# Loading x and the first projection's weights in six pairs of transfers, with the rope angles and the sum over x moved later

## The reference, cut to what matters

```python
h = rms_norm(x, attn_pre_g[0])
a = h @ w_a                                   # 1024 -> 384 + 256 + 64
cq, ckv, kr = jnp.split(a, [384, 640], axis=-1)
q  = (rms_norm(cq, g_q) @ w_uq) ...           # rope on part of it
kv = (rms_norm(ckv, g_kv) @ w_ukv) ...
ang = positions[..., None] * inv              # rope tables
cos, sin = jnp.cos(ang), jnp.sin(ang)
```

## Time and profile before

| | us |
|---|---|
| median of 3 runs | 982.19 |
| lowest and highest run | 981.73, 982.43 |
| span of the profiled execution | 980.3 |
| TensorE busy in the span | 958.4 (98%) |
| DVE busy | 720.6 (74%) |
| ACT busy | 542.4 (55%) |

### The profile page before, as it was taken

One profiled execution on the slowest core, in us unless ns is written; L12 is line 12 of the kernel. 1 busy time (PEld: TensorE's weight loads), 2 busy tenths in 40 slices (PEclk: granted clock), 3 DMA queues, 4 the chain that ended last, 5 costly groups with the idle time before them and its releaser, 6 DMA issues.

```text
span 980.3 us, 18888 instructions
## 1 busy us (share of the span) xinstructions
PE 958.4 (98%) x7971; PEld 923.9 (94%) x7971; DVE 720.6 (74%) x1340; ACT 542.4 (55%) x837; POOL 25.4 (3%) x54
## 2 busy tenths in 40 slices
PE   8999999999999999999999999999999999999997
PEld 8889999999998988899999997998999999999996
DVE  7965897777658777698879788555654879888653
ACT  7554664454447366565444545456755567666542
POOL 0300000000000000000000000000220000000000
PEclk9999999999999999999999999999999999999999
DMA  8536376766744734368767882653343545555621
GB/s 298 190 116 238 128 266 255 255 251 225 295 172 168 266 129 140 116 212 304 265 251 267 331 315 76 245 185 116 111 149 132 199 157 207 181 203 184 216 87 43
DMA packets 27588, 194.72 MB, mean 199 GB/s; under 512 B 3056, under 2 KB 3184, under 8 KB 4592
## 3 DMA queue, kind: packets, MB, share of 16 engines
q1 hardware_dynamic: 27504, 193.51, 54.7%
HBM read 192.45 MB, written 1.05 MB: 197 GB/s over the span
## 4 chain that ended last, share of the span: by engine, by line
PE 89%; ACT 4%; DVE 4%; issue 2%; DMA 1%; POOL 0%; SPq 0%; DVEq 0%; ACTq 0%
PE bank L508 25%; PE bank L509 24%; PE bank L514 23%; PE bank L639 2%; PE bank L665 2%; PE bank L569 2%; PE bank L563 2%; ACT s_whi L906 2%; PE bank L564 2%; PE bank L528 2%; PE bank L535 1%; PE bank L529 1%; PE bank L649 1%; DVE s_wlo L1382 1%; DMA s_xT<-in_xT 1%
## 5 line engine op out<-in xcount | busy, mean ns | idle before, releaser
L1382 DVE TENSOR_TENSOR s_wlo<-s_raw,s_whi 128x512 fp32r<-128x512 f32 (+1 forms) x364 | 372.3, 1065 | 138.1 <-ACT s_whi L906 137.9
L906 ACT ACTIVATE s_whi<-s_raw 128x1024 fp32r<-128x1024 f32 (+2 forms) x233 | 304.8, 1335 | 215.6 <-PE bank L514 205.9
L508 PE MATMUL bank<-s_hh,s_whi 128*128 128x256 f32 x1400 | 393.6, 281 | 1.1 <-DVE s_wlo L1382 0.7
L509 PE MATMUL bank<-s_hl,s_whi 128*128 128x256 f32 x1400 | 387.6, 277 | 0.0
L514 PE MATMUL bank<-s_hh,s_wlo 128*128 128x256 f32 x1383 | 382.8, 277 | 0.0
L508 PEld LDWEIGHTS bank<-s_hh,s_whi 128*128 128x128 f32 x1400 | 263.3, 188 | 6.9 <-issue 5.9
L509 PEld LDWEIGHTS bank<-s_hl,s_whi 128*128 128x128 f32 x1400 | 263.2, 188 | 0.1
L514 PEld LDWEIGHTS bank<-s_hh,s_wlo 128*128 128x128 f32 x1383 | 259.8, 188 | 0.0
L508 PE MATMUL bank<-s_ph,s_whi 128*128 128x256 f32 x528 | 146.4, 277 | 0.0
L509 PE MATMUL bank<-s_pl,s_whi 128*128 128x256 f32 x528 | 145.8, 276 | 0.0
L514 PE MATMUL bank<-s_ph,s_wlo 128*128 128x256 f32 x516 | 142.5, 276 | 0.0
(11 more groups left out here) (238 smaller groups left out, 1285.3 us busy)
## 6 DMA issues: line engine op xcount, KB each, us to landing
s_raw<-in_gu SPq DMA_DIRECT2D x44, 1024.0 KB, 4.9
s_raw<-in_dn SPq DMA_DIRECT2D x33, 1024.0 KB, 4.9
s_raw<-in_wada SPq DMA_DIRECT2D x24, 1024.0 KB, 5.7
s_raw<-in_up SPq DMA_DIRECT2D x22, 1024.0 KB, 4.9
s_raw<-in_wo SPq DMA_DIRECT2D x8, 1024.0 KB, 4.9
s_raw<-in_win_g SPq DMA_DIRECT2D x8, 1024.0 KB, 4.9
s_raw<-in_mla SPq DMA_DIRECT2D x4, 1024.0 KB, 5.4
s_raw<-in_wkv_v SPq DMA_DIRECT2D x4, 1024.0 KB, 4.9
```

The costliest lines, as they stand in the source:

```text
L508: e.matmul(out, hi, xh[:, k, :], start=first, stop=False, skip_group_check=True)
L509: e.matmul(out, hi, xl[:, k, :], start=False, stop=False, skip_group_check=True)
L906: e.activation(whi[w % SPLIT][:, at], raw[p % RAW][:, at], ACT.Copy).then_inc(S.hi.tick((w, c0)), 1)
L1382: e.tensor_tensor(wlo[s][:, at], raw[p % RAW][:, at], whi[s][:, at].bitcast(F32), ALU.subtract).then_inc(S.lo.tick((i, j), (i, "all")), 1)
```

## The change

x and the weights of `wa` pieces 0 and 1 come in six pairs of transfers, one pair for each of the chunks 0, 1, 2, 3 and one for 4 and 5 and for 6 and 7; ACT and DVE wait for the pair that they need. The positions move behind x and come in a transfer of their own behind the sixth pair. `WARM` is 12 instead of 16. On ACT the squares of x come between the high parts of piece 2, and sine and cosine behind them. On DVE `x_low` follows each low part of pieces 0 and 1; the angle steps come with chunks 6 and 7 and between the low parts of piece 2, and the sum of squares between and behind those. TensorE's `sums("x0", 7)` moves from behind `lead` to the middle of output tile 5. The layout in on-chip memory behind `xT` stays where it was.

```diff
@@ -39,8 +39,10 @@
...
 NFIRST = 9
-WARM = 16
-FRONT = 16 + T
+WARM = 12
+FRONT = 16
+BLOCKS = ((0, 1), (1, 2), (2, 3), (3, 4), (4, 6), (6, 8))
+BLOCK_OF = {k: b for b, (k0, k1) in enumerate(BLOCKS) for k in range(k0, k1)}
 MLA = ([("wuk", i) for i in range(4)] + [("wuq", i) for i in range(12)] +
@@ -327,9 +329,9 @@
...
         wlo = [sb(f"wlo{i}", [P, PIECE * P], F32R) for i in range(SPLIT)]
-        x_front = sb("xT", [P, FRONT + 8 * T])
-        xT = x_front[:, FRONT:].rearrange("p (a b) -> p a b", a=8)
-        shift(960 + 1024 - 4 * FRONT)
+        x_front = sb("xT", [P, FRONT + 9 * T])
+        xT = x_front[:, FRONT:FRONT + 8 * T].rearrange("p (a b) -> p a b", a=8)
+        shift(960 - 4 * FRONT)
         hh = sb("hh", [P, 8, T], F32R)
@@ -352,7 +354,7 @@
...
         banks = [ctx.enter_context(nc.psum_tensor(f"bank{i}", [P, 512], F32)) for i in range(8)]
-        cosb, sinb, posi = adacc[:, 0:T], adacc[:, T:2 * T], x_front[:, FRONT - T:FRONT].bitcast(I32)
+        cosb, sinb, posi = adacc[:, 0:T], adacc[:, T:2 * T], x_front[:, FRONT + 8 * T:FRONT + 9 * T].bitcast(I32)
         sqb = [yb[:, 2 * i:2 * i + 2, :] for i in range(4)]
@@ -403,10 +405,11 @@
...
         S.cols_in = signal("cols_in", 16)
-        S.x_in = [signal(f"x_in{i}", 16) for i in range(2)]
+        S.x_in = [signal(f"x_in{i}", 16) for i in range(len(BLOCKS))]
+        S.pos_in = signal("pos_in", 16)
         S.relb_in, S.relm_in, S.c_in = signal("relb_in", 16), signal("relm_in", 16), signal("c_in", 16)
         S.raw_in = [signal(f"raw_in{i}", 16) for i in range(RAW)]
-        S.first_in = signal("first_in", 16)
+        S.first_in = [signal(f"first_in{i}", 16) for i in range(len(BLOCKS))]
         S.out_stored = signal("out_stored", 16)
@@ -448,8 +451,13 @@
...
             q = Once(e, counted)
-            first = FRONT + 2 * T
-            e.dma_start(x_front[:, 0:first], a["xT"][:, 0:first]).then_inc(S.x_in[0].tick("x"), 16)
+            for b, (k0, k1) in enumerate(BLOCKS):
+                x_at = slice(FRONT + k0 * T if k0 else 0, FRONT + k1 * T)
+                piece, w_at = k0 // 4, slice(k0 % 4 * 512, k0 % 4 * 512 + (k1 - k0) * 512)
+                src = a["wa"][:, piece * PIECE * P * P:(piece + 1) * PIECE * P * P].rearrange("a (p n) -> (a p) n", p=P)
+                e.dma_start(x_front[:, x_at], a["xT"][:, x_at]).then_inc(S.x_in[b].tick("x"), 16)
+                e.dma_start(raw[piece][:, w_at], src[:, w_at]).then_inc(S.first_in[b].tick(b), 16)
+            e.dma_start(x_front[:, FRONT + 8 * T:], a["xT"][:, FRONT + 8 * T:]).then_inc(S.pos_in.tick("pos"), 16)
             last = {name: WEIGHTS[of[-1]] for name, of in OF.items()}
@@ -460,11 +468,7 @@
...
                 dst = raw[i % RAW]
-                if i == 0:
-                    e.dma_start(dst[:, 0:1024], src[:, 0:1024]).then_inc(S.first_in.tick(0), 16)
-                    e.dma_start(x_front[:, first:], a["xT"][:, first:]).then_inc(S.x_in[1].tick("x"), 16)
-                    e.dma_start(dst[:, 1024:2048], src[:, 1024:2048]).then_inc(S.raw_in[0].tick(0), 16)
-                else:
+                if i >= 2:
                     e.dma_start(dst[:, 0:k * P], src).then_inc(S.raw_in[i % RAW].tick(i), 16)
@@ -536,7 +540,7 @@
...
 
-            def tiles(name, n, m, nk, xh, xl, made, b, by, last=0, seven=None):
+            def tiles(name, n, m, nk, xh, xl, made, b, by, last=0, seven=None, between=None):
 
@@ -551,6 +555,8 @@
...
                                 event if k == nk - 1 else None, name in HALVED and j == 0 and k == 1 and n % HALVED[name] == 0)
+                        if between is not None and j == 0 and k == 3:
+                            between()
 
@@ -681,9 +687,8 @@
...
             lead("wa", 4, 8, hh, hl, "h0", (0, 1), S.dve_out)
-            sums("x0", 7, acc=1)
             tiles("wa", 4, 1, 8, hh, hl, "h0", 2, S.dve_out)
-            tiles("wa", 5, 2, 8, hh, hl, "h0", 3, S.dve_out)
+            tiles("wa", 5, 2, 8, hh, hl, "h0", 3, S.dve_out, between=lambda: sums("x0", 7, acc=1))
             tiles("wuk", 0, 2, 2, cqh, cql, "cq", 4, S.dve_out)
@@ -896,8 +901,9 @@
...
                 p = WEIGHTS[w]
-                if w == 0 and i < 2:
-                    q.wait_ge(S.first_in, 0)
+                if w < 2:
+                    b = BLOCK_OF[4 * w + c0 // 4]
+                    q.wait_ge(S.first_in[b], b)
                 else:
@@ -1018,37 +1024,32 @@
...
             def x_high(k):
-                q.wait_ge(S.x_in[0 if k < 2 else 1], "x")
+                q.wait_ge(S.x_in[BLOCK_OF[k]], "x")
                 e.activation(hh[:, k, :], xT[:, k, :], ACT.Copy, scale=col("pre0", k)).then_inc(S.xhi.tick(("h0", k)), 1)
...
 
-            x_high(0)
-            x_high(1)
-            hi_part(2)
-            hi_part(2)
-            for k in range(2, 6):
+            for k in range(4):
                 x_high(k)
-            hi_part(2)
-            hi_part(2)
-            x_high(6)
-            x_high(7)
+                hi_part(2)
+            for k in (4, 6):
+                x_high(k)
+                hi_part(2)
+                x_high(k + 1)
+            hi_part(3)
+            x0_square(0)
+            x0_square(1)
+            hi_part(3)
+            x0_square(2)
+            x0_square(3)
             q.wait_ge(S.rot, "angle")
...
             e.activation(cosb, tmp[0][:, :], ACT.Sin, scale=-1.0, bias=epsc[:, 1:2]).then_inc(S.trig.tick("cos"), 1)
-            x0_square(0)
-            hi_part(2)
-            hi_part(2)
-            x0_square(1)
-            x0_square(2)
-            hi_part(3)
-            x0_square(3)
-            hi_part(3)
             log_tables()
@@ -1520,7 +1521,7 @@
...
                 if i == 0:
-                    q.wait_ge(S.x_in[0], "x")
+                    q.wait_ge(S.pos_in, "pos")
                     m = e.tensor_copy(r_[:, :], posi)
@@ -1537,26 +1538,25 @@
...
             def x_low(k):
-                q.wait_ge(S.x_in[0 if k < 2 else 1], "x")
+                q.wait_ge(S.x_in[BLOCK_OF[k]], "x")
                 low_scaled(xT[:, k, :], col("pre0", k), hh[:, k, :], hl[:, k, :], "h0", k)
 
-            angle(0)
-            angle(1)
-            x_low(0)
+            for k in range(8):
+                lo_part(2)
+                x_low(k)
+                if k >= 6:
+                    angle(k - 6)
+            lo_part(3)
             angle(2)
-            x_low(1)
-            lo_part(1)
             angle(3)
-            lo_part(1)
-            for k in range(2, 6):
-                x_low(k)
-                angle(k + 2)
-            lo_all(1)
-            x_low(6)
-            x_low(7)
-            lo_all(2)
-            for i in (1, 2, 3):
-                square_sum("x0", i, sqv[i])
+            lo_part(3)
+            for i in range(4, 8):
+                angle(i)
+            lo_part(3)
+            square_sum("x0", 1, sqv[1])
+            lo_part(3)
+            square_sum("x0", 2, sqv[2])
+            square_sum("x0", 3, sqv[3])
             fold("x0")
@@ -2098,7 +2098,7 @@
...
     pos = np.broadcast_to(f["positions"][0].astype(np.int32).view(np.float32)[None, :], (P, T))
-    o["xT"] = np.concatenate([o["cols"][:, :NFIRST], np.zeros((P, FRONT - T - NFIRST), np.float32), pos, x], axis=1)
+    o["xT"] = np.concatenate([o["cols"][:, :NFIRST], np.zeros((P, FRONT - NFIRST), np.float32), x, pos], axis=1)
     wa = f["mla_w_a"][0]
```

## The result

| | before | changed |
|---|---|---|
| median of 6 runs each, us | 982.58 | 986.97 |
| lowest and highest run | 981.73, 983.17 | 983.93, 990.59 |
| span of the profiled execution | 980.3 | 981.7 |
| time of the changed kernel's profiled execution | | 983.93 |
| TensorE busy, DVE busy, ACT busy in the span | 958.4, 720.6, 542.4 | 956.2, 721.5, 542.9 |

The ratio is 1.0043 [1.0024, 1.0063]: slower by 0.4%, where 983.1 and "no difference" had been forecast, and outside the range. Two things stand out. The runs of the changed kernel spread over 6.7 us, those of before over 1.4. And the profiled execution is the fastest of the six, only 1.4 us of span above that of before. So these two profiles show 1.4 of the 4.4 us, and the rest must be looked for in other executions.

The account below looks back on a forecast made before the run. TensorE, busy 98% of the span, bounds the kernel; only its waits can change. The 3.7 us won in `lead` are lost at `wuk`; scores come 0.95 later, so span 980.3 gives 981.3, plus 1.9 is 983.1; range 980.8 to 985.2.

Parts of the forecast that it names:

- TensorE's lead: TensorE in `lead`: it ends at 17.6 instead of 21.3, taken alone a gain of 3.7 us.
- the two new waits: TensorE stands 1.7 us before the sums of x in tile 5 and 2.8 us before `wuk`.
- The chain from the fold: DVE and ACT to `wuk`: fold ends 23.3, R 25.0, `low_rank(0)` 1.4 later, `wuk` at 30.5 instead of 29.91.
- read as 16 us: Skill's 2.0 us fixed per DMA: eight more transfers, one behind the other, would cost some 16 us; not adopted.
- the transfers "at nothing": Start of the queue: bytes give the landings, thirteen issues cost nothing, the queue stays full, piece 2 still at 14.9.
- the last weights of pair 4: Transfers in `lead`: pair 4 ends at 2312 KB, interpolated to land at 10.2 us.
- The row it had leaned on: Price of 1 KB rows: 158.5 KB transfer landed at 15.3 while the queue moved 467 GB/s, so nothing extra.
- rival A: From pair 4's landing: small transfers are paid for, 1.6 us for piece 2, so 984.8; chance 0.15.
- the first product: TensorE's start on x: the first product at about 5.6 instead of 7.8 us.
- The scores: TensorE's first scores, after DVE's stretch behind `wuk`: 44.55 instead of 43.60, later by 0.95 us.
- rival B: Wait before `wuk`: TensorE's clock falls from 2.4 to 1.2 GHz, up to 1.5 us more, so 984.6; chance 0.04.
- Behind the scores: Rest of the kernel: nothing found that could give the delay back, since each stage waits for TensorE.

Follow-up runs that it names:

- r6: Changed kernel's new order of work with the five old transfers of the kernel before: 986.54 us, ratio 1.0040.
- r9: Changed kernel with unread matmuls in all three waits (7 before the sums of x, 11 before `wuk`, 9 before the scores): 984.46 us, ratio 1.0015.
- r2: Changed kernel with 16 unread matmuls at the start instead of 12: 987.15 us, ratio 1.0044.
- r4: Changed kernel with 7 unread matmuls before the sums of x and 11 before `wuk`: 984.98 us, ratio 1.0024.
- r8: Kernel before with 6 unread matmuls in its wait before the first scores: 983.38 us, ratio 1.0003.
- r13: Kernel before with piece 1 sent as four transfers with rows of 2 KB: 981.47 us, one run.
- r17: Kernel before with piece 0 sent as four transfers with rows of 2 KB: 982.26 us, one run.
- r10: Changed kernel with positions behind pair 1, angle steps early, sine and cosine ahead of piece 2's high parts: 986.94 us, ratio 1.0042.
- r11: Changed kernel with four pairs of transfers instead of six: 988.29 us, ratio 1.0053.
- r15: Changed kernel with four pairs of transfers instead of six, run once more: 988.57 us, one run.
- r16: Kernel before with the six later chunks of x as six transfers with rows of 1 KB: 983.50 us, one run.
- r18: Kernel before with piece 0 as four, piece 1 as four and x's later chunks as six transfers: 983.96 us, one run.
- r1: Changed kernel run again, unchanged: 987.18 us, ratio 1.0039.
- r5: Kernel before with the six pairs of transfers, old order of work, positions in the first pair: 983.70 us, ratio 1.0008.
- r7: Changed kernel with 9 unread matmuls in the wait before the first scores: 985.30 us, ratio 1.0021.
- r14: Kernel before with piece 1 as four transfers of 32 partitions each, rows of 8 KB: 983.03 us, one run.

## Why the prediction was wrong

**What held.** TensorE's lead came (`lead` was over at 18.4 instead of 21.3, forecast 17.6) and was lost again at `wuk`; the two new waits stand where they had been put. The chain from the fold is right link by link. Counted from piece 2's landing, the fold ended after 8.2 us (24.72 - 16.53) and 8.4 had been forecast (23.3 - 14.9); from the end of the fold to `wuk` it was 7.4, forecast 7.2; the waits were 1.5 and 2.5, forecast 1.7 and 2.8. r6, whose expectation came from the same chain with the old landings, has fold and `wuk` where it had put them. The rule of the Trainium skill ("DMA: Bandwidth & Descriptors", the anatomy of one DMA), read as 16 us, is far from it: eight transfers more cost 1.65 us at piece 2. The page fits its 2.0 us to one DMA on GpSimd's path, and this is SP's queue, kept full.

**The step that failed first: the transfers "at nothing".** The prediction took bytes alone to give the landings and the last weights of pair 4 at 10.2; they landed at 10.9, and piece 2 at 16.53 instead of 14.9. Its reason, that the queue would not run dry, was true from 6 us on and not enough. The row it had leaned on, 158.5 KB with rows of 1268 bytes, does not bear on the 467 GB/s beside it: by the packet records none of its packets starts in that stretch, 15 to 16 us, which is rows of 4 and 8 KB; its own had run from 12 to 15 us, took 55 ns each, and that is 369 GB/s. This is rival A at its own size, 1.6 us. Of its reason, a price for each transfer, the runs show only a part: 0.55 us is the price of 1024 more packets with shorter rows, and the rest is slow packets, idle engines at the start and a later last part, whose cause stays open. `wuk` was 1.6 late by it (32.12 for 30.5). Also part of this: the first product at 6.2 instead of 5.6. The scores came at 46.44 for 44.55: the same 1.6, and 0.3 from where DVE and POOL meet.

**The step that failed second: the clock, rival B at 0.04.** The forecast itself had waits of 1.7 and 2.8 us and gave the fall a chance of 0.04 because it had not come in 2.0 us before. But it looked at one execution. A wait is a chance of a fall in each execution: the changed kernel's falls came behind waits of 1.84 to 2.49 us, and filling its waits took them away (r9). The change shortened one such wait, in `lead`, added two and made the one before the scores longer (1.87 for 1.34). That last one, which does it in r2 and r4 (low for 6.8 us; r4's two groups are 4 us apart), was not in rival B at all. Its sign, matmuls 0.22 apart behind 30 us, is not in the first profile, and yet the falls are in the median. Against the kernel before, +0.95 had been forecast and +4.0 to +4.4 came, and the larger part of what is missing is this: 2.6, less the 0.7 that before had in its own median. (Of the 3.9 between 986.97 and 983.1, another 0.4 is that the forecast stood on 982.19 for the kernel before, which was 982.58 beside it.)

**Behind the scores** the prediction found nothing that could give a delay back. The scores are 2.84 us later than before, and the span only 1.4 longer: against ACT's marks of before the delay is 2.8 at 48 us, 2.1 at 152 and 1.5 at 818. That is no merit of the change. The same drops, of 0.5 to 0.9 us each and at the same two places (between 100 and 152 us, and between 700 and 818), stand in executions of the old order: r8 goes from +0.2 to -0.5, r13 from +0.1 over -0.4 to -0.9, r17 from +0.7 to -0.1. They come and go from one execution to the next. What makes them is open, and so is how much of the 2.8 reaches the end in the mean.

Together: +0.95 forecast; 1.4 by the spans of two executions at full clock and 1.6 to 2.2 by the medians at full clock, so 0.5 to 1.3 for the transfers and the 0.3 of DVE and POOL; and 1.9 net for the clock.

## What to carry to other kernels

Making TensorE early on one resource only moves its wait to the next one, and each wait of some 2 us is a chance of a lower clock in every execution, so a profile without a fall does not price it: look at the spread of the runs and their mean clocks, and fill such waits with unread matmuls before anything else is judged. In a full queue count packets beside bytes when a load is split: by their median packets rows of 1 and 2 KB moved 16% and 8% slower than rows of 8 KB, and a quarter slower with the slow packets that were among them. Price the whole sum for several executions, not for one.

## What the runs showed of the hardware

- The clock fell behind waits of 1.84, 1.85 and 1.88 us at the scores (r2, r10, r4), of 2.48 and 2.49 at `wuk` (r6, r10, r11, r15) and of 2.02 and 2.15 in `lead` (r16, r18). It fell 0.1 to 1.4 us behind the first matmul after the wait, once (r11) 0.3 us ahead of it, and came back after 3.4 us at `wuk` and in `lead`, and after 6.8 at the scores. No fall came behind waits of 2.48 and 1.87 in the changed kernel's first profile, of 2.49 in r1, of 2.21 in r5, of 2.34 in r7, and of 2.00 in that of before.
- Which execution gets a fall goes with how long its unread matmuls at the start had run at 1.2 GHz. In eleven profiled executions the clock had first risen by 5.9 us, and one of them had a fall (r15); in nine it rose between 6.0 and 7.3, and seven of them had one (not r5 and r7). r6's 24 unread matmuls took 5.37 us, those of the first profile 4.39. The kernel does not set this time: with the start of the changed kernel it was 4.1 to 6.7 us. Why the two go together no run shows.
- A transfer to only 32 partitions is slow even with rows of 8 KB. r14, while piece 1 was moved:

```profile
10.00:12.00 2.00, 1.09 (x10) 0.89 (x8) 2.00 (x7) 1.50 (x4) 0.00 (x0) 1.00 0.99 217
12.00:14.00 2.00, 0.97 (x8) 1.00 (x9) 2.00 (x6) 1.97 (x7) 0.00 (x0) 1.00 0.99 221
```

It is half the rate of before (418 and 414) at a DMA share of 0.99; piece 2 landed 3.3 us later, and yet the one run took 983.03 us. The four transfers of 256 KB landed 1.0 to 1.7 us apart.
- The 16 parts of a transfer drift apart, and not by one rule: piece 2's last part came 0.7 us behind its median part before and in r13, r17 and r18, 1.05 in the changed kernel's first profile, 1.45 in r16 and 2.5 in r11. A landing is the slowest part's.
